# A decoder layer on one core: the second up pass and the down pass of the expert mixer run in one stage, with 256 instead of 192 gathered tokens

## The reference

```python
qh = (xc @ w_query).reshape(chunk, PEER_HEADS, D_KEY)
v1, i1 = lax.top_k(s1, 16); v2, i2 = lax.top_k(s2, 16)        # scores against two sets of 128 keys
top, pos = lax.top_k(v1[..., :, None] + v2[..., None, :], 16)  # 128 chosen experts for each token
g = softmax(top)
act = gelu(einsum('nd,nhkd->nhk', xc, expert_u[idx]))
out = einsum('nhk,nhkd->nd', g * act, expert_v[idx])
```

## Time and profile before

| what | value |
|---|---|
| median of 3 runs | 2011.68 us (2007.05 to 2012.56) |
| profiled execution, its own time | 2011.93 us |
| its span | 2010.3 us |
| granted clock of TensorE, mean share of full speed | 0.977 |
| busy share: PE, DVE, POOL, ACT | 95%, 69%, 56%, 43% |
| pass one, first to last matmul | 617.3 to 1028.4 us |
| pass two | 1028.4 to 1494.3 us |
| downs | 1512.5 to 2004.7 us |

### The profile page before, as it was taken

The page is one execution under the profiler, slowest core; times in us unless marked ns, Lnnn a source line. Parts: engine busy times, 40 slices in busy tenths (PEclk is TensorE's granted clock), DMA queues, the critical chain, the costliest instruction groups (busy, mean ns, idle before and its releaser), DMA issues.

```text
span 2010.3 us, 39023 instructions
## 1 busy us (share of the span) xinstructions
PE 1904.8 (95%) x14702; PEld 1805.8 (90%) x14702; DVE 1390.1 (69%) x2528; ACT 856.2 (43%) x1119; POOL 1119.5 (56%) x755
## 2 busy tenths in 40 slices
PE   7988988888999999999999999999989999999998
PEld 6977764358999999999999999999989999999998
DVE  3669665432589888964446776465638999999996
ACT  4233664412213454556566555344433333333331
POOL 3323222223225888886768888778864555665630
PEclk8999999889999999999999999999998999999999
DMA  5434878761123777776867898998989999999993
GB/s 166 78 107 150 284 255 284 245 214 63 64 106 126 221 228 233 219 230 224 303 220 273 307 348 313 397 338 310 338 290 306 323 361 348 354 358 335 358 332 113
DMA packets 253534, 508.80 MB, mean 253 GB/s; under 512 B 51041, under 2 KB 172962, under 8 KB 232642
## 3 DMA queue, kind: packets, MB, share of 16 engines
q1 hardware_dynamic: 202930, 369.56, 54.3%
q0 software_dynamic: 44032, 134.35, 18.4%
q10 hardware_dynamic: 6416, 2.78, 1.0%
HBM read 442.77 MB, written 63.73 MB: 252 GB/s over the span
## 4 chain that ended last, share of the span: by engine, by line
PE 72%; DVE 10%; POOL 6%; DMA 4%; ACT 4%; issue 2%; DVEq 1%; SPq 1%; ACTq 0%; POOLq 0%
PE pair L1552 20%; PE pair L1553 20%; PE pair L1554 19%; PE pair L1883 4%; DVE conv L1082 3%; POOL w_lo L651 2%; PE pair L1697 2%; POOL v_rows L662 2%; DMA act<-acts 2%; DMA acts<-act_out 1%; POOL picked_a L655 1%; PE pair L1709 1%; DVE pair L1437 1%; DVE w_lo L1491 1%; PE pair L1749 1%
## 5 line engine op out<-in xcount | busy, mean ns | idle before, releaser
L1552 PE MATMUL pair<-x_hi,w_hi 128*128 128x256 f32 (+2 forms) x2560 | 752.5, 294 | 28.0 <-DVE x_lo L1038 16.2
L1553 PE MATMUL pair<-x_lo,w_hi 128*128 128x256 f32 (+2 forms) x2560 | 742.5, 290 | 0.0
L1554 PE MATMUL pair<-x_hi,w_lo 128*128 128x256 f32 (+2 forms) x2560 | 741.0, 289 | 0.0
L1552 PEld LDWEIGHTS pair<-x_hi,w_hi 128*128 128x128 f32 x2560 | 487.0, 190 | 33.5 <-issue 18.8
L1553 PEld LDWEIGHTS pair<-x_lo,w_hi 128*128 128x128 f32 x2560 | 486.4, 190 | 0.2
L1554 PEld LDWEIGHTS pair<-x_hi,w_lo 128*128 128x128 f32 x2560 | 484.7, 189 | 0.0
L1552 PE MATMUL pair<-a_hi,w_hi 128*128 128x352 f32 x1024 | 332.5, 325 | 12.9 <-DVE w_lo L1491 9.7
L662 POOL DMA_INDIRECT v_rows<-in_v_t,at_row x192 | 199.4, 1039 | 238.0 <-DVE pair L1437 205.2
L1553 PE MATMUL pair<-a_lo,w_hi 128*128 128x352 f32 x1024 | 331.5, 324 | 0.0
L1554 PE MATMUL pair<-a_hi,w_lo 128*128 128x352 f32 x1024 | 331.2, 323 | 0.0
L651 POOL TENSOR_TENSOR w_lo<-w_raw,w_hi 128x1024 fp32r<-128x1024 f32 x116 | 275.7, 2399 | 87.5 <-ACT w_hi L922 87.4
(11 more groups left out here) (219 smaller groups left out, 2735.6 us busy)
## 6 DMA issues: line engine op xcount, KB each, us to landing
w_raw<-in_u_t SPq DMA_DIRECT2D x85, 1024.0 KB, 5.6
v_raw<-in_u_t SPq DMA_DIRECT2D x43, 1024.0 KB, 5.3
w_raw<-in_v_t SPq DMA_DIRECT2D x128, 256.0 KB
v_raw<-in_v_t SPq DMA_DIRECT2D x128, 256.0 KB
gates<-g_out SPq DMA_DIRECT2D x11, 2048.0 KB, 10.7
act<-acts SPq DMA_DIRECT2D x64, 352.0 KB, 5.9
g_in<-gates SPq DMA_DIRECT2D x16, 1408.0 KB, 10.5
acts<-act_out SPq DMA_DIRECT2D x64, 288.0 KB, 7.1
```

The costliest lines, as they stand in the source:

```text
L1552: te.matmul(out, s_hi, m_hi, start=start, stop=False)
L1553: te.matmul(out, s_hi, m_lo, start=False, stop=False)
L1554: return te.matmul(out, s_lo, m_hi, start=False, stop=stop)
```

## The change

- 256 tokens are gathered (NS = 256), exactly those of pass one, so there are 256 rows k instead of 192, and 288 columns in the downs instead of 352. Fewer gate groups are needed: 72.
- All gates are made in pass one, four groups in each step from t = 46 to 63 (in `up`, at kd = 2 and kd = 6 of both halves). The first group stands right behind the last `turn_slots` (t = 45).
- Pass two and the downs are one stage of 68 slots: slot s does up(64 + s), s < 64, and then down(s - 4), s >= 4. The activations of pass two stay in SBUF (`act`), where they are gated in place; nothing of them is stored or loaded.
- There are three places for high and low weights, the third over the tokens of `x_hi` and `x_lo` that pass two doesn't read. `u` and `v` have two raw buffers each.
- From t = 64 on DVE splits u(65) to u(68) and every u with t % 3 != 0, and all `v`; POOL splits the other `u`.
- Rows are added from slot 2 to slot 65, 4.13 in a full slot (256 over 62). In POOL's list a slot is: the fetches for the first half of its rows, the split of the next `u` if it is POOL's, the fetches for the rest. In DVE's it is: `add_block`, `split_u` of the next `u` if it is DVE's, half of the rows, `gate_acts`, `split_v`, `low_acts`, `add_block`, the rest of the rows.
- In the front, the convolution's sigmoid moves ahead of `keep_output(0)` and `finish_conv` from slots 22 to 25 to slots 17 to 20; in the out projection `high_w` comes before the square of a block, and the last one before the root.

```diff
-EXTRA = 64
-NS = P + EXTRA
+NS = FIRST
 ND = N - NS
-GATES_FROM, GATES_PER_STEP = 47, 2
-FETCH_FROM, UNITS_FROM, ROWS_FROM = 58, STEPS + 1, STEPS + 7
+GATES_FROM, GATES_PER_STEP = 46, 4
+FETCH_FROM = 58
+BESIDE = 4
+ENDS = STEPS + BESIDE
...
-    return t % 4 == 0 if ROWS_FROM <= t < SPLIT_FROM else t >= SPLIT_FROM and t % 3 != 0
+    return t > STEPS and (t <= STEPS + BESIDE or t % 3 != 0)
...
+    highs = [by_blocks(w_hi[:, 0, :]), by_blocks(w_hi[:, 1, :]), x_hi[:, :, 0:WCOL]]
+    lows = [by_blocks(w_lo[:, 0, :]), by_blocks(w_lo[:, 1, :]), x_lo[:, :, 0:WCOL]]
...  SP, behind pass one
+            store_beside(STEPS - 1)
+            wait_low_u(sp, STEPS)
+            load_u(STEPS + 2)
             for parity in range(2):
+                sp.wait_ge(g_stored[parity], 16 * ((NG + 1 - parity) // 2))
+            load_gates(0, 0)
+            for parity in range(2):
+                sp.wait_ge(acts_stored[parity], 16 * STEPS // 2)
+            load_v(1)
+            load_gates(1, 1)
+            for slot in range(ENDS):
+                if slot + 3 < STEPS:
+                    wait_low_u(sp, STEPS + slot + 1)
+                    load_u(STEPS + slot + 3)
+                c = slot + 1 - BESIDE
+                if 0 <= c < STEPS - 2:
                     sp.wait_ge(v_lo_done, c + 1)
+                    load_v(c + 2)
...  POOL
+            for slot in range(ENDS):
+                for k in range(PIECE * slot, PIECE * slot + PIECE):
+                    if k < AHEAD:
                         fetch_unit(k)
+                mine = rows_added_at(slot)
+                for k in mine[:len(mine) // 2]:
                     fetch_ahead(k)
+                if slot + 1 < STEPS and not on_vector(STEPS + slot + 1):
+                    split_u(STEPS + slot + 1)
+                for k in mine[len(mine) // 2:]:
+                    fetch_ahead(k)
...  ACT
+            for slot in range(ENDS):
+                c = slot + 1 - BESIDE
+                if slot + 1 < STEPS:
+                    high_u(STEPS + slot + 1)
+                if slot < STEPS:
+                    gelu_out(STEPS + slot, 0)
+                    gelu_out(STEPS + slot, 1)
+                if 0 <= c < STEPS:
+                    high_v(c)
+                for step in gated_at(slot):
+                    high_a(step)
...  PE
+            for slot in range(ENDS):
+                if slot < STEPS:
+                    up(STEPS + slot)
+                if slot == TURN_FIRST:
+                    turn_rows(0)
+                if slot >= BESIDE:
+                    down(slot - BESIDE)
```

## The result

The changed kernel took 2028.68 us (median of 4 runs, 2026.33 to 2030.99) beside 2010.33 us for the kernel before: a ratio of 1.0092, interval 1.0079 to 1.0105. It is slower by 0.9%, and the 114 us that PE could have saved are gone. The forecast was 2013 us, range 1930 to 2065, so the time lies in the range, 15.7 us above the forecast.

The account below looks back on a forecast made before the run. PE set the pace nearly everywhere, POOL in pass two and the new slots. Pass one to 1063.4, slots 0 to 3 to 1101.8, then 839, 38.4 and 26.6 give 2005.8; with 5.6 and 1.6, 2013 us, range 1930 to 2065.

Parts of the forecast that it names:

- PE's saving: Whole kernel at PE's pace: 82 us from 288-column chunks, 18.2 at the border, 14 from fewer gate groups; 114 us.
- The front: Before pass one: moved DVE instructions and splits change the time by -8 to +8 us, taken as 0.
- Pass one: 38 more gate groups add 33.4 us, a one-hot wait 3.6, less 2.0 of POOL wait; ends at 1063.4.
- Slots 0 to 3: Start of fused stage: ups 25.6 us, wait at u(67) 9.7, slower clock 3.1; together 38.4, bounds 26 and 50.
- Full slots: Slots 4 to 60: POOL's issues, splits and holds set 14.8 us a slot, against PE's 12.8.
- the head start: Slots 4 to 60: 5 us that POOL may be late before PE stands, taken off 844 us.
- POOL's idle time there is pauses, not `add_row`: Sign for the full slots: POOL idles only in pauses, not waiting for DVE's `add_row`; no size given.
- POOL never waits for `row_used`: Full slots: POOL is behind, so its wait for DVE counts as nothing in the 44.4 us for three slots.
- PE keeps the pace: Rival for the slots: POOL's holds fall into its waits, 12.8 us a slot, 1904 us; chance 0.14.
- half of the holds hidden: Rival for the full slots: 40.1 us for three, 13.4 each, 1933 us, up to 1970 if fewer; chance 0.16.
- DMA binds: Rival for the full slots: 340 GB/s where 356 are wanted, 13.4 us a slot, about 1933 us; chance 0.04.
- DVE becomes the bound: Rival for the full slots: DVE waits for POOL's split and late rows, 15.7 us a slot, 2065 us; chance 0.24.

Follow-up runs that it names:

- e6: Changed kernel with all `u` splits of pass two on DVE and DVE's `u` and `v` splits in halves: 1896.01 us, ratio 0.9422.
- e8: Kernel before with only the three front edits (earlier sigmoids, `finish_conv` and last `high_w`): 2008.39 us, ratio 0.9978.
- e5: The changed kernel unaltered, measured again on the second chip: 2003.93 us (10 runs), ratio 0.9971 to the kernel before.
- e1: Changed kernel with all `u` splits of pass two on DVE, none on POOL: 1934.94 us, ratio 0.963.
- e3: Changed kernel with each DVE split of `u` and `v` made as two instructions of 128x1024: 1959.47 us, ratio 0.9747.
- e7: Changed kernel with POOL splitting the next `u` ahead of all its fetches of the slot, instead of between them: 2003.94 us, ratio 0.9962.
- e9: The changed kernel unaltered, measured a third time, on the third chip: 2039.64 us (4 runs), ratio 1.0154 to the kernel before.
- e2: Changed kernel fetching only each eighth unit, its value standing for all eight (another result, only timed): 1938.25 us, ratio 0.9646.
- e10: Changed kernel with all `u` splits of pass two on DVE and splits in halves, on the third chip: 2026.42 us, ratio 1.0101.
- e11: As e10, on the same chip, plus the load of u(67) issued ahead of the gate-store wait and the gate and v(1) loads: 2026.21 us, ratio 1.0093.
- e12: Kernel before with the loops of its downs on PE, ACT and SP written out, on the third chip: 2009.41 us, ratio 0.9998.

## Why the prediction was right, and where it was not

**PE's saving**: right in size. e6 gains 114 us, 2010.3 less 1896.0. That this is just the 114 of the forecast is partly chance: the forecast's own time at PE's pace, with the waits at the border, was 1904 (a span of 1902.4), and of the 6.4 us that e6's span lies below that the front gave 4.5 and slots of 12.75 in place of 12.8 us 2.9, while pass one took 1.2 more.

**The front** was taken as 0 with bounds of 8; it gave 4.4 us (e8), 6.4 in the first profile, 2 to 8 over the twelve.

**Pass one**: forecast 443.2 us from its first matmul to the first at 288 columns, measured 445.1 in the first profile and 445.0 in e5. The wait for the first one-hot piece was 3.5 us, forecast 3.6.

**Slots 0 to 3**: forecast 38.4, measured 38.7 and 39.2 from the first slot's gelu to the fifth's. PE's wait for `w_lo` of DVE there was 6.9 and 8.3 us, forecast 9.7. The clock took more than the 3.1 us of the forecast: 0.88 over the 44 us of the second window is 5.3 at most. So two errors cancel in part.

**Full slots**: POOL as the bound at 14.8, 14.72 with the head start. Measured 15.04 in the first profile and 14.60 in e5. That POOL binds is shown from four sides on the first two chips: taking its splits away (e1), shortening its holds (e3), both (e6), and reordering it (e7, no effect). Its terms, issues, splits and holds, came to within 0.7 us each of the forecast in e5. The signs named were there: an issue of 1.22 us in the mean in the first profile and 1.26 in e5, each third slot longer by 1 to 12 us with a wait for `w_lo`, DVE busy 81 and 88%. One sign, "POOL's idle time there is pauses, not `add_row`", was there in e5 (6.4 us in 720), and not in the first profile (53.9 in 770).

**Where the 15.7 us come from.** Against the profiled 2026.3 us they are 13.3: front -6.4, pass one +1.9, slots 0 to 3 +0.3, 57 slots of 15.04 in place of 14.72 +18.2, which leaves -0.7 for the rest. So the term that was mis-sized is the full slot, and in it "POOL never waits for `row_used`": in the first profile POOL waits 1.05 us a slot for DVE, behind the late gelus, while its holds are fewer (6.9 us in three slots, forecast 8.6). Without the late gelus the term was 0.12 us too long, 6.8 in all. So the two profiles of one program differ by 25.1 us in this term, for a reason that the forecast did not have; that the sum still came within 15.7 us of the first measurement owes 6.4 us to the front and 6.8 to a term that was too long, and that much is luck. The sum stood within 0.8% of the first measurement and 0.5% of e5, and 1.3% below e9.

**The sign** was given as faster 0.46, slower 0.38. The first measurement and e9 say slower, e5 says faster by 0.3%: the case lay on the border, where 0.3 us a slot decide it, but the side that I held for the likelier one was the wrong one for the first measurement.

**The rivals.** "PE keeps the pace", "half of the holds hidden" and "DMA binds" did not happen; e6 shows the DMA at 356 GB/s with PE unhindered. "DVE becomes the bound" did not happen at 15.7 a slot, but its mechanism is what e2 ran into: I had 36.4 us for DVE in the sum and POOL's hold on it, 4.8, only in the rival, although the first rows had shown both directions.

**The rule of the Trainium skill** (SBUF — State Buffer, section "SBUF: two separate sides"), an exclusive lock for the whole instruction: e3 is its test. With instructions of 1.22 us for 2.29 the holds of POOL fell from 130 to 45 us in 720, as the rule has it. What DVE waited in e5, through two instructions of POOL, is more than one instruction's length.

**Still open**: why PE stalls and gelus come late in these slots on the third chip and in the first profile. Not the third weight place (in e10 and e11 most stalls stand before matmuls that don't read it), not POOL's split (e10 and e11 have none), hardly its holds (34 us in 720 in e11, 130 in e5, which has no stall). The fetching of code is unlikely (e12). Why the stalls keep to the slots 1 mod 3 in the first profile and in e9 (14 of 19 bursts) is open too. Before, written out, is nearly immune on this chip with 350 GB/s in its downs, so that something of the fused slots matters; that semaphore events are lost in the same stretches fits signals that come late, but this was only argued.

## What to carry to other kernels

Before work is fused into one stage, add up every engine's list for the new stage with the pauses, and then the time that it is held by the others: here PE's 12.8 us a slot hid behind POOL's 14.6, though the page had POOL busy for 59% of the span. When DVE and POOL must share ports, cut the long two-input instructions of DVE (e3, 44 us), and keep elementwise work off the engine that issues the gathers (e1, 69 us); together, on the second chip, they gave what the change was meant to give. And measure on more than one chip before a 1% difference is believed.

## What the runs showed of the hardware

- An issue waiting for the ports gets in between two back-to-back instructions of DVE: with splits of 1.22 us only 33 issues of 434 were held for over 0.3 us, with 2.29 us 82 of 413 (e3, e5).
- The hold works on DVE too: two instructions, 0.8 us together otherwise, took 5.9 beside POOL's split of 4.7 (e2), and 11 splits of 2.29 us took 4.8 to 7.3 (e5). At 7.27 DVE had waited through two back-to-back instructions of POOL; it got in between them only where the first of them had itself been held by DVE (8 of 17 in e3, 2 of 18 in e2, none of 16 in e5).
- One program, 2003.9 us on one chip and 2039.6 on another (e5, e9), while another program, before, differs by 0.1% between the same two. Where it is slow, its profile lacks a third of the semaphore events; a profile can also lack events without lost time (e12).
